# Staging expert weights in chunks of 2048 columns through three slots instead of 1024 columns through six

## The reference

```python
def swiglu(h, w_gate, w_up, w_down):
    return (jax.nn.silu(h @ w_gate) * (h @ w_up)) @ w_down

def moe_swiglu(h, w_router, w_gate, w_up, w_down):          # 8 experts, top 2
    logits = (h @ w_router).astype(jnp.float32)
    top_v, top_i = lax.top_k(logits, TOP_K)
    gates = jax.nn.softmax(top_v, axis=-1)
    dense_gate = jnp.sum(jax.nn.one_hot(top_i, N_EXPERTS_2, dtype=jnp.float32) * gates[..., None], axis=-2)
    y = jnp.zeros_like(h)
    for e in range(N_EXPERTS_2):
        y = y + dense_gate[..., e:e + 1].astype(h.dtype) * swiglu(h, w_gate[e], w_up[e], w_down[e])
    return y

def first_block(x, mem, ...):      # three mixers, gates, w_o, layer norm, then
    y_moe = hier_moe(x, w_rg[l], b_rg[l], w_re[l], b_re[l], w1[l], w3[l], w2[l])   # 4 groups x 4 experts
    x = layer_norm(DEEPNORM_ALPHA * x + y_moe, ln2_g[l], ln2_b[l])

def second_block(x, c, ...):
    for l in range(DEPTH_2):       # two layers
        ...
        x = layer_norm_2(ALPHA * x + (1.0 + g_m) * y, ln_g[l, 0], ln_b[l, 0])
        h = x * (1.0 + sc_f) + sh_f
        if l % 2 == 0:
            y = swiglu(h, ffn_w_gate[e], ffn_w_up[e], ffn_w_down[e])
        else:
            y = moe_swiglu(h, moe_w_router[e], moe_w_gate[e], moe_w_up[e], moe_w_down[e])
        x = layer_norm_2(ALPHA * x + (1.0 + g_f) * y, ln_g[l, 1], ln_b[l, 1])
    return x
```

## Time and profile before

| | us |
|---|---|
| median of three runs | 2391.13 (2388.83 to 2392.26) |
| the profiled execution | 2391.78 |
| its span in the profile | 2390.0 |
| PE busy | 2290.8 (96% of the span) |
| VectorE busy | 1633.0 (68%) |
| ScalarE busy | 1294.0 (54%) |
| stage_lo on VectorE, 934 instructions | 1107.2 |
| stage_hi on ScalarE, 934 instructions | 962.4 |
| read from memory | 634.77 MB, 266 GB/s over the span |

### The profile page before, as it was taken

One profiled execution on the slowest core, in us unless ns is written; L12 is line 12 of the kernel. 1 busy time (PEld: TensorE's weight loads), 2 busy tenths in 40 slices (PEclk: granted clock), 3 DMA queues, 4 the chain that ended last, 5 costly groups with the idle time before them and its releaser, 6 DMA issues.

```text
span 2390.0 us, 25914 instructions
## 1 busy us (share of the span) xinstructions
PE 2290.8 (96%) x10482; PEld 1880.9 (79%) x10482; DVE 1633.0 (68%) x1920; ACT 1294.0 (54%) x1563; POOL 0.4 (0%) x6
## 2 busy tenths in 40 slices
PE   8999999997999989789989899999999999999997
PEld 7668877887888876678857788888888888888885
DVE  0376334645898863354432598989899998989895
ACT  1245113104777753254421487777777787878785
POOL 0000000000000000000000000000000000000000
PEclk9999999997999999999999899999999999999999
DMA  9575556655999993044460499999999898989992
GB/s 332 184 253 214 176 194 222 244 220 179 371 340 324 329 327 110 1 176 176 144 226 1 151 388 347 356 345 349 370 340 375 325 377 324 376 326 374 329 374 102
DMA packets 280593, 637.63 MB, mean 267 GB/s; under 512 B 8729, under 2 KB 13710, under 8 KB 280206
## 3 DMA queue, kind: packets, MB, share of 16 engines
q1 hardware_dynamic: 277902, 629.81, 72.5%
q10 hardware_dynamic: 2560, 6.03, 0.7%
HBM read 634.77 MB, written 1.05 MB: 266 GB/s over the span
## 4 chain that ended last, share of the span: by engine, by line
PE 93%; DVE 4%; ACT 2%; DMA 1%; issue 1%; SPq 0%; DVEq 0%; ACTq 0%
PE psum L1715 55%; PE psum L1498 19%; PE psum L1490 5%; PE psum L1725 2%; PE psum L1592 2%; PE psum L1738 2%; PE psum L1805 1%; DMA ring<-w_in 1%; PE psum L1598 1%; DVE stage_lo L1349 1%; PE psum L1610 1%; PE psum L1433 0%; DVE arena L557 0%; DMA ring<-w_in_in 0%; ACT arena L544 0%
## 5 line engine op out<-in xcount | busy, mean ns | idle before, releaser
L1349 DVE TENSOR_TENSOR stage_lo<-ring,stage_hi 128x1024 fp32r<-128x1024 f32 (+1 forms) x934 | 1107.2, 1217 | 111.9 <-ACT stage_hi L923 90.1
L923 ACT ACTIVATE stage_hi<-ring 128x1024 fp32r<-128x1024 f32 (+1 forms) x934 | 962.4, 1055 | 284.0 <-PE psum L1715 234.2
L1715 PE MATMUL psum<-stage_hi,x_hi 128*128 128x512 f32 (+1 forms) x1344 | 529.1, 394 | 14.2 <-DVE x_lo L1331 11.5
L1715 PE MATMUL psum<-stage_hi,x_lo 128*128 128x512 f32 (+1 forms) x1344 | 522.3, 389 | 0.0
L1715 PE MATMUL psum<-stage_lo,x_hi 128*128 128x512 f32 (+1 forms) x1344 | 521.0, 388 | 0.0
L1715 PEld LDWEIGHTS psum<-stage_hi,x_hi 128*128 128x128 f32 x1344 | 253.2, 188 | 64.1 <-issue 11.9
L1715 PEld LDWEIGHTS psum<-stage_hi,x_lo 128*128 128x128 f32 x1344 | 253.1, 188 | 53.0
L1715 PEld LDWEIGHTS psum<-stage_lo,x_hi 128*128 128x128 f32 x1344 | 253.5, 189 | 49.2
L1715 PE MATMUL psum<-stage_hi,h_hi 128*128 128x512 f32 x664 | 259.9, 391 | 4.7 <-DVE h_lo L1388 4.7
L1715 PE MATMUL psum<-stage_lo,h_hi 128*128 128x512 f32 x664 | 258.5, 389 | 0.0
L1498 PE MATMUL psum<-arena,ring 128*128 128x256 f32 x1024 | 229.8, 385 | 6.2 <-DVE arena L1296 4.3
(11 more groups left out here) (214 smaller groups left out, 1831.6 us busy)
## 6 DMA issues: line engine op xcount, KB each, us to landing
ring<-moe_w_gate_in SPq DMA_DIRECT2D x56, 2048.0 KB, 9.2
ring<-moe_w_up_in SPq DMA_DIRECT2D x56, 2048.0 KB, 9.3
ring<-moe_w_down_in SPq DMA_DIRECT2D x56, 2048.0 KB, 9.0
ring<-w_in SPq DMA_DIRECT2D x48, 2048.0 KB, 10.1
ring<-ada_w_in SPq DMA_DIRECT2D x15, 2048.0 KB, 8.0
ring<-w_in_in SPq DMA_DIRECT2D x14, 2048.0 KB, 9.8
mixer_tiles<-ada_w_in SPq DMA_DIRECT2D x9, 2048.0 KB, 7.9
mixer_tiles<-w_in_in SPq DMA_DIRECT2D x6, 2048.0 KB, 13.5
```

What stands on the lines that cost most here:

```text
L923: act.activation(chunk_view(stage_hi, f, side, p, c), chunk_source(f, side, p, c), ACT.Copy)\
L1349: dve.tensor_tensor(chunk_view(stage_lo, f, side, p, c), chunk_source(f, side, p, c), chunk_view(stage_hi, f, side, p, c).bitcast(F32), AL ...
L1715: ins = pe.matmul(dst, a, b, start=start, stop=stop)
```

## The change

The staging tiles keep their size (6 x 1024 = 3 x 2048 columns) and are cut into three slots. A G or U panel has 2 chunks (`PARTS`) of 4 rows of 512 columns (`ROWS`), a D panel 2 chunks of 2 rows of 1024. Everything that counted chunks is counted anew: the loads' waits, the splitting of h, the points at which tokens, copies and additions are done. PE's matmuls stay the same, in the same order, with one semaphore wait and one signal per chunk, so half as many. Four constants do not merely halve: the tokens of a routed pass are split behind 2 large chunks instead of 3 small ones; in the second pass chunk 0 of G(0) waits for two of x_lo's four parts instead of one; the first chunk of G(p+1) ahead of the turn there is twice as long; and h_hi there comes one chunk behind it instead of two.

```diff
@@
-STAGES = 6
+STAGES = 3
+ROWS = 4
+PARTS = KT // ROWS
@@ build
-    stage_hi = ctx.enter_context(nc.sbuf_tensor("stage_hi", [P, STAGES, 1024], F32R))
+    stage_hi = ctx.enter_context(nc.sbuf_tensor("stage_hi", [P, STAGES, ROWS * PANEL], F32R))
...
@@ unit_steps
-        chunk = lambda side, p: [("chunk", side, p, c) for c in range(4 if side != "D" else pairs[p] // P)]
+        chunk = lambda side, p: [("chunk", side, p, c) for c in range(PARTS if side != "D" else pairs[p] // (2 * P))]
...
-            n = 4 if routed else 1
+            n = PARTS if routed else 1
@@ chunk_view, chunk_source
-        rows, width = (2, f["pairs"][p]) if side != "D" else (1, D)
+        rows, width = (ROWS, f["pairs"][p]) if side != "D" else (2, D)
@@ h_point
-            make[order[count[("chunk", "U", p, 3)] + STAGES - 1]] = p
-            before_turn = count[("chunk", "G", p + 1, 3 if f["routed"] else 0) if p < last
-                                else ("chunk", "D", p - 1, 3)]
-
-            at = max(before_turn + (STAGES if f["routed"] else 2), count[("chunk", "U", p, 3)] + STAGES - 1)
+            make[order[count[("chunk", "U", p, PARTS - 1)] + STAGES - 1]] = p
+            before_turn = count[("chunk", "G", p + 1, PARTS - 1 if f["routed"] else 0) if p < last
+                                else ("chunk", "D", p - 1, f["pairs"][p - 1] // (2 * P) - 1)]
+
+            at = max(before_turn + (STAGES if f["routed"] else 1), count[("chunk", "U", p, PARTS - 1)] + STAGES - 1)
@@ unit_loads
-                    wait = (lane.chunk_lo, lane.c0 + u * f["chunks"] + 4 * (k - FF_SLOTS + 1))
+                    wait = (lane.chunk_lo, lane.c0 + u * f["chunks"] + PARTS * (k - FF_SLOTS + 1))
@@ ScalarE's body
-                    if count[q] == (2 if f["routed"] else 0) and u == 0:
+                    if count[q] == (1 if f["routed"] else 0) and u == 0:
                         take_tokens(u, "gather_first")
@@ VectorE's body
-                    if n == (2 if f["routed"] else 0) and u == 0:
+                    if n == (1 if f["routed"] else 0) and u == 0:
                         take_tokens(fill)
-                    if n == STAGES + 3:
+                    if n == STAGES + 1:
                         if u:
                             add_output(jobs + (pos[("scatter", 0)] - 1))
@@ PE's body
                         if first and side == "G" and p == 0:
-                            pe.wait_ge(lane.x_lo_set, fill + c * f["x_parts"] // 4 + 1)
+                            pe.wait_ge(lane.x_lo_set, fill + (c + 1) * f["x_parts"] // PARTS)
...
-                            for k in range(2):
+                            for k in range(ROWS):
                                 for t in range(nt):
                                     part = slice(t * P, (t + 1) * P)
                                     ins = products([psum[:, b0 + t, 0:pairs[p]]],
-                                                   (x_hi[:, 2 * c + k, part], x_lo[:, 2 * c + k, part]),
+                                                   (x_hi[:, ROWS * c + k, part], x_lo[:, ROWS * c + k, part]),
```

More of the change, by code:

```diff
@@ L233, in build @@
         pass
[L234 to L235 removed]
+    stage_hi = ctx.enter_context(nc.sbuf_tensor("stage_hi", [P, STAGES, ROWS * PANEL], F32R))
+    stage_lo = ctx.enter_context(nc.sbuf_tensor("stage_lo", [P, STAGES, ROWS * PANEL], F32R))
     x_hi = ctx.enter_context(nc.sbuf_tensor("x_hi", [P, KT, T], F32R))
@@ L522, in build @@
             if k >= len(order) - FF_SLOTS:
-                last = ("chunk", *order[k], 3 if order[k][0] != "D" else f["pairs"][order[k][1]] // P - 1)
+                last = ("chunk", *order[k], PARTS - 1 if order[k][0] != "D" else f["pairs"][order[k][1]] // (2 * P) - 1)
                 freed[k % FF_SLOTS] = (chunk_lo, f["c0"] + f["chunks"] * (f["n"] - 1) + f["count"][last] + 1)
@@ L954, in body @@
                         p = make[q]
-                        act.wait_ge(lane.job, jobs + pos[("chunk", "U", p, 3)])
+                        act.wait_ge(lane.job, jobs + pos[("chunk", "U", p, PARTS - 1)])
                         if p0 + p:
@@ L1779, in body @@
                         if side == "D":
-                            for t in range(nt):
-                                part = slice(t * P, (t + 1) * P)
-                                ins = products([psum[:, 2 * t + m, :] for m in range(2)],
-                                               (h_hi[:, c, part], h_lo[:, c, part]),
-                                               [(hi[:, 0, m * PANEL:(m + 1) * PANEL],
-                                                 lo[:, 0, m * PANEL:(m + 1) * PANEL]) for m in range(2)],
-                                               p == 0 and c == 0, p == len(pairs) - 1 and c == pairs[p] // P - 1)
+                            for r in range(2):
+                                j = 2 * c + r
+                                for t in range(nt):
+                                    part = slice(t * P, (t + 1) * P)
+                                    ins = products([psum[:, 2 * t + m, :] for m in range(2)],
+                                                   (h_hi[:, j, part], h_lo[:, j, part]),
+                                                   [(hi[:, r, m * PANEL:(m + 1) * PANEL],
+                                                     lo[:, r, m * PANEL:(m + 1) * PANEL]) for m in range(2)],
+                                                   p == 0 and j == 0, p == len(pairs) - 1 and j == pairs[p] // P - 1)
                         else:
                             b0 = 6 if side == "U" else 4 if width == T else 4 + p % 2
-                            for k in range(2):
+                            for k in range(ROWS):
                                 for t in range(nt):
```

3 lines of the change are left out of this document (1 added, 2 removed).

## The result

The changed kernel took 2403.3 us, median of five runs (2395.88 to 2404.06), against 2391.13 for the kernel before (five runs, 2388.83 to 2395.59): ratio 1.0038, 95% interval 1.0025 to 1.0052. A later repetition gave 2398.74 us against 2391.45, ratio 1.0037 (1.0023 to 1.0051). The medians differ by 12.2 us the first time and by 7.3 the second; both ratios say some 9 us (6 to 12). So it is slower, by more than the 0.2% that can be told from no change; the forecast was 2396.6 us, with 2392 to 2409 as its range.

A forecast was written before the change was run, and what follows sets the result against it. PE was taken to set the pace, so cheaper staging gains 0. Terms of 2.55, 0.9 and 0.7 us, plus 0.9 for late loads and 0.5 for jitter, gave +5.5 us on the median 2391.13: 2396.6 us, range 2392 to 2409.

The forecast's parts named there:

- likeliest case: The forecast itself, chance 0.66: from +1 to +9 us, centre 5.5, 2392 to 2400 us.
- Durations: Staging instructions: 1.92 us on ScalarE, 2.29 on VectorE; busy time down 93 and 70 us, worth 0 on PE's path.
- faster case: Half as many PE semaphore waits, 467 fewer: at 25 ns each -12 us, 2383 us; chance 0.07.
- Steady pair: Three slots in a routed pair of panels: tightest at G's first chunk, slack 0.4 us, 72 times, cost 0.
- first rival: G's slack is not there: PE waits 0.2 to 0.3 us at each pair, 2409 to 2417 us; chance 0.12.
- What PE waits for now: Before the change, expert matmuls and weight loads waited 28 us in 13 places, 0.7 us in two for stage_lo.
- Start of pass 2: PE's wait for x_lo, 11.5 us, grows by longer hi and lo and a second part of x_lo: +2.55 us.
- Last panel of pass 2: The 256-wide panel holds PE only 2.88 us on the G chunk, so PE waits for stage_lo: +0.7 us.
- Ends of the routed passes: PE's wait for h_lo after the turn grows by 0.45 us, twice: +0.9 us.
- Late loads: Panel loads issued later: cost 0 in the median, +0.9 us for one late D panel, bounds 0 and +6.
- One of the prediction's own signs: The prediction is wrong if "stage_hi waits for DMA" grows to much more than now.
- rival on loads: Landings grow past D's window plus slack: 1 to 2 us in 5 to 8 stretches, 2400 to 2410 us; chance 0.11.

The follow-up runs named there:

- pass 2 alone: 2048-column chunks in pass 2 only, passes 1 and 3 as in the kernel before: 2395.52 us against 2392.13, ratio 1.0012.
- after: The changed kernel's profile; the profiled execution took 2395.88 us, the fastest of its five.
- before: The profile of the kernel before the change, 1024-column chunks in six stage slots; median 2391.13 us.
- pass2_small: The changed kernel with pass 2 back at 1024-column chunks through six slots: 2394.44 us, ratio 1.0013 to the kernel before.
- best: 2048-column chunks with four ring slots for loads in passes 1 and 3, 1024-column chunks in pass 2: 2386.55 us, ratio 0.9976 to the kernel before.
- ring4_large: The changed kernel with four ring slots instead of three for panel loads in the two routed passes: 2390.86 us, ratio 0.9997 to the kernel before.
- again: The changed kernel without any edit, for a second profile: 2398.74 us, ratio 1.0037 to the kernel before.
- pass3_large: 2048-column chunks in pass 3 only, the rest as in the kernel before: 2395.2 us against 2392.13, ratio 1.0009.
- pass1_large: 2048-column chunks in pass 1 only, the rest as in the kernel before: 2391.14 us against 2392.13, ratio 0.9991.
- hlo_early: The changed kernel with h_hi and h_lo made one chunk earlier in the routed passes: 2397.16 us, ratio 1.0026 to the kernel before.

## Why the prediction was right, point by point

The side and the range came out: slower, by some 9 us where 5.5 was forecast. The likeliest case, 2392 to 2400 us, holds 2398.74 but not the first median of 2403.3. And the sum is near by luck as well: one term was several times too small, and a gain that nobody had forecast made up for part of it.

- **Durations.** 1.92 and 2.29 us, and no gain from them: right. Busy time fell by 42 us on VectorE and 68 on ScalarE, not by 70 and 90: neighbouring small chunks overlap by about 0.1 us, and half of those overlaps went as well. PE's pace across chunks didn't change, so the faster case, half as many semaphore waits, has no trace at all. The Trainium skill ("Perfetto Trace Analysis", "Optimizing Scalar/DVE Operations") has it that breaking instructions up may let the work finish sooner where these engines hold others up; 1.0012 for pass 2 alone agrees, its first chunk being the larger one.
- **Steady pair.** Slack 0.4 us at G's first chunk, 72 times: held. In pass 3 of after PE starts on that chunk 0.51 us (median) behind the end of its stage_lo, the handover included; in before it was 4.2, as worked out. PE's products wait for stage_lo in two places in after, 1.1 us (one of 0.2 before), one of them the last panel of pass 2, the other behind a late load in pass 1. The first rival is false.
- **What PE waits for now.** The prediction read 28 us in 13 places from the earlier trace rows. That list counts the wait of a product and that of its weight load each for itself, so it is seven places, and some 19 us on the products. No term of the sum hangs on it, but one of the four waits for h_lo is in the middle of pass 1, behind the late panel of the earlier trace rows: late loads had already reached PE.
- **Start of pass 2.** Forecast +2.55, measured +2.8 (14.3 against 11.5). Large chunks in pass 2 alone make it 14.05, in pass 1 alone 11.8; so pass 2's own part is +2.5, as worked out. In pass2_small and best it is 11.8.
- **Last panel of pass 2.** Forecast +0.7, measured +0.6: 0.86 us at 1188.83 in after, 0.23 before. The stretch grew by only 0.1: the half-clock time that before had near 1048 us isn't there in after.

```profile
1045.00:1050.00 5.00, 3.88 (x12) 3.10 (x13) 1.06 (x2) 0.00 (x0) 0.00 (x0) 0.76 0.55 208
```

```profile
1045.00:1050.00 5.00, 3.90 (x17) 3.24 (x18) 1.05 (x2) 0.00 (x0) 0.00 (x0) 1.00 0.96 367
```

The first is a window of before, the second the same of after; the granted clock is 0.76 and 1.00.

- **Ends of the routed passes.** Forecast a wait of 1.85 us. At the end of pass 3 in after it is 1.78, and in ring4_large 1.76 and 1.78: right, where the last panel is on time. At the end of pass 1 in after it was 2.59, since that panel was late, and a clock fall followed: +2.8 us in place of +0.45. The term held; that late loads meet it just there is what the sum left out.
- **Late loads.** This term was mis-sized: +0.9 us for one place, "Cost 0 in the median". Measured by what ring4_large takes away: 2.9 us in pass 3 and, with what followed at its end, 3.8 us in pass 1. The step set D's window of 9.35 us and a slack of 0.8 against the median landing of 9.3 us, and priced what exceeds them by one row of before. Window and slack were about right: the down panels that cost PE time in pass 3 of after landed in 10.1 to 10.5 us. But the change had moved the threshold, not the loads: of the pass's 168 panels 32 took 10 us or more in before and none made PE wait, in after 39 did and seven, all down panels, made it wait. The spread of landings had to be held against the new window, not the late ones counted under the old. One of the prediction's own signs shows it weakly: ScalarE's waits for expert loads grew from 43.7 to 52.7 us (63.7 in again). The rival on loads had the mechanism half right: landings didn't grow (9.3, 9.5, 8.8), they only ceased to be covered, and each cost 0.4 to 0.6 us of weight-load waiting in pass 3 of after and not 1 to 2.
- **What nobody forecast** is mixer 2, 3.7 us shorter. Without it the change would have cost some 11 us by the stretches, and the forecast been only half of that. Why the gap in mixer 2 closed is open.

## What to carry to other kernels

For a ring of loads, write down the loop: the landing, and everything until the slot is free again, against the ring's number of panels times the consumer's time for one; a longer instruction at the end of that path costs nothing until the slowest landings no longer fit, and then, as here, another ring slot mends it where another stage slot doesn't. Size the reserve in front of a busy engine by the longest interruption of the stager, here a unit's head, not by the steady pair. Before reading a stretch's length as waiting, look for a clock fall in it. And where nothing is covered, at the start of a pass, the first chunk should be the smallest.

## What the runs showed of the hardware

- VectorE's 2.0 us gap ("issue") behind pass 1 appears with small chunks in pass 1 and doesn't with large ones. There VectorE has just jumped over the code for units with more than 128 tokens, which is shorter with large chunks; the traffic of one of the two instruction queues is less as well, 44 packets in before and 37 in after (packets, MB, share; first before, then after):

```profile
q14 instruction: 44, 0.36, 0.0%
```

```profile
q14 instruction: 37, 0.30, 0.0%
```

 That the gap is the loading of code behind the jump is only argued; no run tested it. The packets of the whole kernel don't sort the profiles: pass3_large has 38 and the gap, pass1_large 41 and none.

- At the end of pass 1 PE's wait for h_lo was followed by full clock where it was 1.4 to 2.0 us (nine profiles). At 2.3 to 2.6 us the clock fell to 0.50 in three profiles, and at 2.6 and 2.8 us in two others it didn't. At the end of pass 3 a wait of 1.78 us was followed by a fall in hlo_early and pass2_small and by none in after, again and pass3_large. So the length of the wait alone doesn't decide. Which layer norm matmuls meet half clock shifts between kernels too (5.38 us against 3.69 for the same sixteen), so a change's cost can come back or double in a stretch that it didn't touch.
